# Four consecutive rows of the gate and up matrices to a partition, with the gather taking every fourth column

## The reference

```python
def _hier_moe(h, w_r1, b_r1, w_r2, b_r2, w_gate, w_up, w_down):
    hf = h.reshape(B * T, D)                       # 256 x 1024, normalised, scaled by g_ffn
    g_sel = jnp.argmax(g_logits, axis=-1)          # a group of experts for each token
    top_p, top_i = lax.top_k(e_prob, EXPERT_TOPK)  # two experts of that group
    ...
    hid = jax.nn.silu(jnp.einsum('nd,edf->nef', hf, w_gate)) * jnp.einsum('nd,edf->nef', hf, w_up)
    hid = hid * combine[..., None].astype(hid.dtype)
    out = jnp.einsum('nef,efd->nd', hid, w_down)
```

## Time and profile before

| what | value |
|---|---|
| median of 3 runs | 1009.08 us |
| the profiled execution's own time | 1009.04 us |
| its span in the trace | 1007.7 us |
| mean granted TensorE clock | 0.997 |
| PE busy | 987.0 us, 98% of the span |
| DVE busy | 681.9 us, 68% |
| ACT busy | 586.0 us, 58% |
| mean DMA rate | 205 GB/s |

### The profile page before, as it was taken

One profiled execution on the slowest core, in us unless ns is written; L12 is line 12 of the kernel. 1 busy time (PEld: TensorE's weight loads), 2 busy tenths in 40 slices (PEclk: granted clock), 3 DMA queues, 4 the chain that ended last, 5 costly groups with the idle time before them and its releaser, 6 DMA issues.

```text
span 1007.7 us, 16344 instructions
## 1 busy us (share of the span) xinstructions
PE 987.0 (98%) x6730; PEld 892.9 (89%) x6730; DVE 681.9 (68%) x1021; ACT 586.0 (58%) x856; POOL 45.2 (4%) x57
## 2 busy tenths in 40 slices
PE   6999999999999999999999999999999989999997
PEld 6998988999999999889898888998999978888885
DVE  5866767677555555585575766566556679998886
ACT  6574577665434343474585545776444558777773
POOL 4101000000000000010010001100000000000001
PEclk9999999999999999999999999999999989999999
DMA  9994533456565555564443334554656919999994
GB/s 260 278 308 136 169 124 126 160 174 205 174 202 177 201 178 199 185 203 161 135 165 127 124 126 126 170 170 128 189 187 209 325 52 317 365 368 372 371 369 175
DMA packets 168248, 206.31 MB, mean 205 GB/s; under 512 B 11431, under 2 KB 143118, under 8 KB 168174
## 3 DMA queue, kind: packets, MB, share of 16 engines
q1 hardware_dynamic: 159598, 196.01, 59.7%
q0 software_dynamic: 2224, 6.07, 2.0%
q10 hardware_dynamic: 6352, 3.19, 1.2%
HBM read 201.56 MB, written 4.73 MB: 205 GB/s over the span
## 4 chain that ended last, share of the span: by engine, by line
PE 91%; DMA 4%; DVE 3%; ACT 1%; issue 1%; POOL 0%; SPq 0%; DVEq 0%; ACTq 0%; POOLq 0%
PE bank L624 78%; DMA ring<-in_w_down 1%; PE bank L761 1%; PE bank L817 1%; PE bank L807 1%; DMA ring<-in_w_in 1%; DVE w_lo L600 1%; PE bank L3048 1%; PE bank L2722 1%; DMA ring<-in_w_out 1%; PE bank L2777 1%; PE bank L2739 1%; DMA x<-in_x 1%; ACT w_hi L592 0%; PE bank L3088 0%
## 5 line engine op out<-in xcount | busy, mean ns | idle before, releaser
L600 DVE TENSOR_TENSOR w_lo<-ring,w_hi 128x1024 fp32r<-128x1024 f32 (+1 forms) x302 | 423.1, 1436 | 178.3 <-ACT w_hi L592 178.0
L592 ACT ACTIVATE w_hi<-ring 128x1024 fp32r<-128x1024 f32 (+1 forms) x302 | 357.6, 1225 | 186.9 <-PE bank L624 144.5
L624 PE MATMUL bank<-xT_hi,w_hi 128*128 128x256 f32 x896 | 253.0, 282 | 0.0
L624 PE MATMUL bank<-xT_lo,w_hi 128*128 128x256 f32 x896 | 250.3, 279 | 0.0
L624 PE MATMUL bank<-xT_hi,w_lo 128*128 128x256 f32 x896 | 250.3, 279 | 0.0
L624 PEld LDWEIGHTS bank<-xT_hi,w_hi 128*128 128x128 f32 x896 | 168.7, 188 | 2.5 <-issue 1.6
L624 PEld LDWEIGHTS bank<-xT_hi,w_lo 128*128 128x128 f32 x896 | 170.1, 190 | 0.0
L624 PEld LDWEIGHTS bank<-xT_lo,w_hi 128*128 128x128 f32 x896 | 168.6, 188 | 0.8 <-issue 0.2
L624 PE MATMUL bank<-w_hi,xT_hi 128*128 128x512 f32 (+1 forms) x208 | 77.6, 373 | 0.3 <-ACT cmp_in L1313 0.3
L624 PE MATMUL bank<-w_hi,xT_lo 128*128 128x512 f32 (+1 forms) x208 | 76.1, 366 | 0.0
L624 PE MATMUL bank<-w_lo,xT_hi 128*128 128x512 f32 (+1 forms) x208 | 76.0, 365 | 0.0
(11 more groups left out here) (549 smaller groups left out, 1789.0 us busy)
## 6 DMA issues: line engine op xcount, KB each, us to landing
ring<-in_w_in SPq DMA_DIRECT2D x54, 1024.0 KB, 5.2
ring<-in_w_down SPq DMA_DIRECT2D x31, 1024.0 KB, 7.0
ring<-in_w_gate SPq DMA_DIRECT2D x40, 512.0 KB, 7.2
ring<-in_w_up SPq DMA_DIRECT2D x40, 512.0 KB, 8.8
ring<-in_w_gate SPq DMA_DIRECT2D x11, 1024.0 KB, 5.4
ring<-in_w_up SPq DMA_DIRECT2D x11, 1024.0 KB, 5.4
ring<-in_w_out SPq DMA_DIRECT2D x8, 1024.0 KB, 5.1
ring<-in_w_mem_kv SPq DMA_DIRECT2D x8, 1024.0 KB, 5.2
```

Source lines behind the costliest of these rows:

```text
L592: act.activation(HIGHS[HI_SLOT[s]][:, k, :], RAWS[SLOT[s]][:, k, :], ACT.Copy).then_inc(w_hi_ready, 1)
L600: vec.tensor_tensor(LOWS[SLOT[s]][:, k, :], RAWS[SLOT[s]][:, k, :], HIGHS[HI_SLOT[s]][:, k, :].bitcast(F32), ALU.subtract).then_inc(w_lo_r ...
L624: ins = pe.matmul(dst, a, b, start=(start and j + m == 0), stop=(stop and j == len(pairs) - 1 and m == 2), **kw)
```

## The change

Within each half of 512 rows, partition p now holds the four consecutive rows 4p to 4p+3, and so chunk k of a half holds the rows p * 4 + k. Each of the 80 transfers of gate or up rows now reads 4 KB in one piece for each partition, and writes it in one piece. Gate and up no longer alternate in the slab: gate takes the first half of each partition's 8 KB, up the second. The moving operand of a product is now two blocks of 256 columns that lie 1024 values apart.

The features of the tokens must be paired alike. The gather therefore takes for chunk k the columns of `x` that start at `k // 4 * 512 + k % 4` and go on in steps of 4, in both the gather (line 3048 before) and the overflow gather (line 3067). The gain is loaded once more in this order, into `g_dealt`, and takes the place of `g_ffn2` in four instructions. The waits for the small loads called "router" count one transfer more.

```diff
+    g_dealt = two("g_dealt", [P, KT])
...
+    def dealt(k):
+        at = k // 4 * (D // 2) + k % 4
+        return slice(at, at + 4 * (P - 1) + 1, 4)
...
-                    k = KT // 2 if step == "second" else 0
+                    h = 1 if step == "second" else 0
                     for a, matrix in enumerate(("w_gate_2", "w_up_2")):
-                        sp.dma_start(RAWS[SLOT[slab]][:, a::2, :],
-                                     expert(matrix).rearrange("a (k p) f -> p (a k) f", p=P)[:, k:k + KT // 2, :])\
+                        sp.dma_start(RAWS[SLOT[slab]].rearrange("p (a k) f -> p a (k f)", a=2)[:, a, :],
+                                     expert(matrix).rearrange("a (h p k) f -> p (a h) (k f)", h=2, p=P)[:, h, :])\
...
+        load(g_dealt[:, :].rearrange("p (h k) -> p h k", h=2),
+             dram["g_ffn_2"][0].rearrange("(h p k) -> p h k", h=2, p=P), "router")
...
-            act.activation(xgs[0][:, k, :], bank[GATHER_BANK[k]][:, :], ACT.Copy, scale=col("g_ffn2", k))\
+            act.activation(xgs[0][:, k, :], bank[GATHER_BANK[k]][:, :], ACT.Copy, scale=g_dealt[:, k:k + 1])\
...
-                ins = mm_(bank[GATHER_BANK[k]][:, :], v[:, t, k * P:(k + 1) * P],
+                ins = mm_(bank[GATHER_BANK[k]][:, :], v[:, t, dealt(k)],
...
-                ins = mm_(bank[6 + k // 4][:, (k % 4) * P:(k % 4 + 1) * P], x[:, t, k * P:(k + 1) * P],
+                ins = mm_(bank[6 + k // 4][:, (k % 4) * P:(k % 4 + 1) * P], x[:, t, dealt(k)],
...
-            w = [v.rearrange("p (k a) f -> p k (a f)", a=2) for v in w_parts(s)]
+            w = [v.rearrange("p (a k) f -> p k a f", a=2) for v in w_parts(s)]
```

More of the change, by code:

```diff
@@ L1769, in _ @@
                     act.activation(xgo[0][:, k, :], bank[6 + k // 4][:, (k % 4) * P:(k % 4 + 1) * P], ACT.Copy,
-                                   scale=col("g_ffn2", k)).then_inc(*moe_act.did("over", k))
+                                   scale=g_dealt[:, k:k + 1]).then_inc(*moe_act.did("over", k))
             if u == 4:
@@ L2415, in _ @@
         vec.wait_ge(*moe_pe.done("router"))
-        vec.wait_ge(loads["router"], 48)
+        vec.wait_ge(loads["router"], 64)
         for t in range(TT):
@@ L2448, in gather_low @@
             vec.wait_ge(*moe_act.done("gather", k))
-            stt_(xgs[1][:, k, :], bank[GATHER_BANK[k]][:, :], col("g_ffn2", k), xgs[0][:, k, :].bitcast(F32),
+            stt_(xgs[1][:, k, :], bank[GATHER_BANK[k]][:, :], g_dealt[:, k:k + 1], xgs[0][:, k, :].bitcast(F32),
                  ALU.mult, ALU.subtract).then_inc(*moe_vec.did("gather", k))
@@ L2527, in _ @@
                     vec.wait_ge(*moe_act.done("over", k | 3))
-                    stt_(xgo[1][:, k, :], bank[6 + k // 4][:, (k % 4) * P:(k % 4 + 1) * P], col("g_ffn2", k),
+                    stt_(xgo[1][:, k, :], bank[6 + k // 4][:, (k % 4) * P:(k % 4 + 1) * P], g_dealt[:, k:k + 1],
                          xgo[0][:, k, :].bitcast(F32), ALU.mult, ALU.subtract).then_inc(*moe_vec.did("over", k))
@@ L3023, in _ @@
         raw_turn(2)
-        pe.wait_ge(loads["router"], 48)
+        pe.wait_ge(loads["router"], 64)
         for k in range(4):
@@ L3079, in tile_product @@
                     pe.wait_ge(*moe_vec.done("gather", k))
-                ins = product(pe, bank[u % 2][:, :], [([v[:, k, :] for v in slots_of(u // PERG)], [v[:, i, :] for v in w])],
+                ins = product(pe, bank[u % 2][:, :], [([v[:, k, :] for v in slots_of(u // PERG)], [v[:, i, :, :] for v in w])],
                               k == 0, k == KT - 1)
```

## The result

The changed kernel is slower by 0.25%: over 14 runs the ratio to the kernel before is 1.0025, with a 95% interval from 1.0017 to 1.0032, about 2.5 us. The medians are 1012.13 us (1010.9 to 1013.8) and 1010.53 us (1008.17 to 1011.16). The forecast had 1.2 us more than the median of the first three runs before, with no measurable change as the likeliest outcome. The direction of both terms came out as forecast. The sizes did not.

A forecast was written before the change was run, and what follows sets the result against it. PE was taken to bound the expert stage until late loads stall it at the end. 1009.04 us, less 2.1 for larger pieces, plus 3.4 for stepped weight loads, gave 1010.3 us; range 1006.4 to 1013.0.

The forecast's parts named there:

- What bounds the kernel: Expert stage: PE bounds it at 8.43 us a tile up to 976.89 us, then late loads hold up the end.
- The gain of larger pieces: Last tiles: 4 KB pieces keep loads ahead of PE, so the stall before turn 19 goes, a gain of 2.1 us.
- The stepped weight loads: Overflow gather: every fourth column doubles a weight load to 213 ns, costing 3.4 us; in the gather it is covered, costing nothing.
- Free steps: Gathers: weight loads don't care about the step, so 1006.9 us, faster; chance 0.28.
- a part price: Gathers: the step costs a factor of 1.2 to 1.6, a result within 0.2%; chance 0.04.
- A factor of 3: Both gathers: a stepped load takes 320 ns, so 1015.6 us, slower; chance 0.12.
- Loads that don't get faster: Expert tiles: larger pieces leave the tail, so 1012.4 us, or 1009.0 if the step is free; chance 0.08.
- The memory limit of 358 GB/s: Expert loads: HBM loads held to about 358 GB/s, a tile taking 8.8 us, so the gain of 2.1 us would be lost.
- Two blocks, gain, added transfer: Moving operand in two blocks, reordered gain and one more small load on ACT's queue: each taken to cost nothing.

The follow-up runs named there:

- the four other traces: Three more traces of the unchanged kernel before and one of it with stepped gathers but 1 KB pieces; late loads cost 1.2, 1.0, 1.6 and 1.2 us.
- the groups of runs: Timed runs of the kernel before and the changed kernel, each sorted into two groups by time; group against group the changed one is 2.9 and 2.7 us slower.
- the ladder: Changed kernel, but chunk k of both gathers reads columns in steps of k + 1, 1 to 8; overflow products took 110, 118, 175, then 225 to 238 ns.
- the first trace: Kernel before, unchanged, the trace the prediction rested on; 173.78 us from the end of the overflow gather to the end of the last product.
- the stepped kernel: Kernel before with its 1 KB pieces, but both gathers read every fourth column; timing only; ratio 1.0044 (1.0028 to 1.006), 4.4 us.
- the second trace of before: Kernel before, unchanged, traced again; 174.05 us from overflow gather's end to last product's end, 172.41 without the clock's second fall.

## Why the prediction was wrong

The terms of the sum were mis-sized, and the mechanisms were right. The step costs more than forecast, 4.0 us instead of 3.4, and the larger pieces give less, about 1.5 instead of 2.1.

*What bounds the kernel.* Right. PE sets the tiles' pace at 8.43 us in all traces, and the late loads are exposed only at the end.

*The gain of larger pieces, forecast 2.1 us.* The mechanism was right: rates of 349 and 410 GB/s for the two sizes of piece, loads ahead of PE, and a chain without DMA. The size was right for the trace that was read, and too large for the usual run: 1.0 to 1.6 us in the four other traces, 1.5 in the mean of all five. The wait of 13.89 us for the last down slab was read as what 1 KB pieces cost. 2.2 us of it were the late last pieces of one slab, and four more traces of kernels with 1 KB pieces don't have them. One trace is one draw of the stall.

*The stepped weight loads, forecast 3.4 us.* This is the term that was mis-sized the other way. The regime and the place were right: the overflow gather had no cover. The factor was taken from DVE as 2.0 on 106 ns, so 213 ns a load, 107 ns more than before. It is 229 ns against 112: 7.34 - 3.57 = 3.8 us. The factor was nearly right, 2.05, though it came from another engine and a step of 16. It belonged on the 112 ns of this gather, and not on the router's 106. The gather, put down at nothing since 213 is under 228, pays as well, because 229 isn't: about 24 products at full clock cost 0.007 us more each, 0.2 us. The rest of its 0.67 us is the clock, which rose 3.9 us into the gather instead of 2.8, and that varies from run to run.

*The sum.* 3.4 - 2.1 = 1.3 us was forecast. By the parts measured it is 3.8 + 0.2 - 1.5 = 2.5 us, and the ratio gives 2.5. The three errors of 0.4, 0.2 and 0.6 us point the same way, and carried the result over the bound of 2.0 us, up to which I had called it no change. That the two figures of 2.5 agree so well is in part luck: the interval of the ratio is 1.7 to 3.2 us, the groups of runs give 2.7 and 2.9, and the gain is a mean of five traces that differ by 1.5 us.

*The rivals.* Free steps are refuted by the ladder, and so is a part price, a factor of 1.2 to 1.6, for a step of 4. A factor of 3 is refuted too, for steps up to 8. Loads that don't get faster are refuted by the windows. The memory limit of 358 GB/s that the Trainium skill states (page "DMA: Bandwidth & Descriptors", section "Where 436 GB/s comes from") does not bind in this trace: the mean over 80 us is 386, of which some 370 are loads.

*Two blocks, gain, added transfer.* Nothing, as forecast. The added transfer took ACT 0.46 us at 664.92, in the slack behind it.

*What I said the profile would show.* The overflow piece was to read 6.9 us and read 7.34. The DMA share was to fall clearly below 1 and did not: it is 1.01 with a rate of 386, since transfers are queued as soon as buffers come free.

*Left open.* Why the last pieces of one slab came 2 us late in the first trace is not known, nor how often that happens. That loads catch up while PE is slow in the gather can be set aside: in the first trace before, the DMA engines moved next to nothing from 813 to 831 us, while SP waited 22.3 us for a free buffer, and the stepped kernel, whose PE came 4 us later to the tiles, issued its last slabs just as late, counted from the end of the overflow gather. What decides whether the clock falls a second time was not tried. The traces show only that the second fall goes with a late rise in the gather.

## What to carry to other kernels

Before taking single columns of a float32 tile in steps as a stationary operand, look at how many moving columns cover the weight load. With 512 a step of 4 costs 3%, with 128 it doubles the product. If rows are dealt to partitions for longer DMA pieces, dealing two at a time gave the rate that PE asks for here, 388 GB/s, and keeps two columns in each line. And where a gain is the remainder of a race between two nearly equal rates, take several traces of the kernel before, since one shows one length of the stall.

## What the runs showed of the hardware

- A weight load of 128 float32 columns, where nothing else limits, is paced by 0.85 ns a column or 1.8 ns a line of 16 bytes, whichever is more: 110, 118, 175 and 233 ns for steps of 1, 2, 3 and 4, and no more up to 8.
- Loads of gate, up and down slabs, with the stores of y_rows, ran at 370 GB/s with 1 KB pieces for two thirds of the bytes, 388 with 2 KB and 386 with 4 KB, the last two held by PE's demand of 389.
- After 20 products of 5 columns each, which follow each other at 106 ns, the granted clock fell to half for 3.4 us (835.3 to 838.7 us in the second trace of before, PE being busy throughout) in seven of twelve traces, and cost 1.6 us in the products behind. Whether these products or the overflow gather ahead of them bring it about was not tried.
- A POOL product of 128 x 2 values that ran beside a DVE sum ended 0.5 to 0.6 us after it, and took 1.12 or 1.51 us as the sum took 0.69 or 1.09.
